# Storing 116-row output tiles as 112 + 4 rows in a one-core streaming encoder step

## The reference, cut to what matters

```python
h = x + jnp.concatenate([attn_out, lru_out], axis=-1) @ w_out
hn = rmsnorm(h, norm_ffn_g)
y = h + jnp.square(jax.nn.relu(hn @ w_up)) @ w_down
...
y_prompt = rmsnorm(yp, final_norm_g)   # (1, 2048, 1024) float32
y_sample = rmsnorm(ys, final_norm_g)   # (1, 32, 1024) float32
```

## Time and profile before

| what | value |
|---|---|
| time of the runs, median of 3 | 2148.1 us (2146.77 to 2150.18) |
| the profiled execution's own time | 2146.69 us |
| its span in the profile | 2144.9 us |
| PE busy / PEld busy | 1983.0 us (92%) / 1878.0 us (88%) |
| DVE busy | 1527.9 us (71%) |
| ACT busy | 1011.2 us (47%) |
| POOL busy | 430.8 us (20%) |
| mean granted clock of TensorE | 0.967 of full speed |
| hardware queue, share of 16 engines | 74.3%, 493.38 MB |
| software queue (POOL's transfers) | 0.8%, 5.67 MB |

### The profile page before, as it was taken

The page is one execution under the profiler, slowest core; times in us unless marked ns, Lnnn a source line. Parts: engine busy times, 40 slices in busy tenths (PEclk is TensorE's granted clock), DMA queues, the critical chain, the costliest instruction groups (busy, mean ns, idle before and its releaser), DMA issues.

```text
span 2144.9 us, 34224 instructions
## 1 busy us (share of the span) xinstructions
PE 1983.0 (92%) x11669; PEld 1878.0 (88%) x11669; DVE 1527.9 (71%) x2183; ACT 1011.2 (47%) x1967; POOL 430.8 (20%) x393
## 2 busy tenths in 40 slices
PE   6789889988987989999999989999999899999994
PEld 6778778777776779999999889999999799999994
DVE  7767867777678788878887966667767766666663
ACT  5555454544544555555555534433335533333331
POOL 3536656555567100100000001000000000000000
PEclk9889999999999999999999999999999999999997
DMA  6767676776755599989999887768878777777761
GB/s 178 226 174 225 176 238 197 209 234 192 214 188 161 167 300 316 317 287 298 345 326 299 290 270 243 230 205 267 272 220 269 239 213 217 216 217 216 216 211 63
DMA packets 396538, 500.91 MB, mean 234 GB/s; under 512 B 27498, under 2 KB 301450, under 8 KB 396394
## 3 DMA queue, kind: packets, MB, share of 16 engines
q1 hardware_dynamic: 394698, 493.38, 74.3%
q0 software_dynamic: 1696, 5.67, 0.8%
HBM read 375.36 MB, written 123.68 MB: 233 GB/s over the span
## 4 chain that ended last, share of the span: by engine, by line
PE 67%; DVE 10%; issue 8%; POOL 7%; DMA 3%; ACT 3%; SPq 1%; POOLq 0%; DVEq 0%; ACTq 0%
PE results L2056 19%; PE tail L2056 14%; PE scores_a L2056 14%; PE results L1840 10%; PE aux L2056 8%; DVE w_lo L1356 2%; PE aux L1960 1%; DVE hn_lo L1497 1%; POOL prob L929 1%; POOL xrow L898 1%; DMA out<-yout 1%; POOL xrow L902 1%; POOL xrow L900 1%; POOL third L900 1%; POOL sumsq L867 1%
## 5 line engine op out<-in xcount | busy, mean ns | idle before, releaser
L1035 ACT ACTIVATE w_hi<-w_raw 128x512 fp32r<-128x512 f32 (+1 forms) x360 | 240.8, 690 | 380.8 <-PE results L2056 160.5
L1507 DVE TENSOR_TENSOR w_lo<-w_raw,w_hi 128x512 fp32r<-128x512 f32 (+1 forms) x360 | 275.7, 779 | 49.0 <-ACT w_hi L1035 48.8
L1840 PE MATMUL results<-xg_hi,w_hi 128*128 128x448 f32 (+1 forms) x560 | 216.1, 386 | 27.6 <-DVE w_lo L1356 21.6
L1840 PE MATMUL results<-xg_lo,w_hi 128*128 128x448 f32 (+1 forms) x560 | 203.5, 363 | 0.0
L1840 PE MATMUL results<-xg_hi,w_lo 128*128 128x448 f32 (+1 forms) x560 | 203.0, 363 | 0.0
L2056 PE MATMUL results<-hn_hi,w_hi 128*128 128x348 f32 x576 | 187.4, 325 | 10.9 <-DVE x L1753 5.0
L971 ACT ACTIVATE w_hi<-raw 128x1024 fp32r<-128x1024 f32 x110 | 116.4, 1058 | 160.3 <-PE results L1840 156.8
L1356 DVE TENSOR_TENSOR w_lo<-raw,w_hi 128x1024 fp32r<-128x1024 f32 x110 | 155.4, 1413 | 49.5 <-ACT w_hi L971 49.5
L2056 PE MATMUL results<-hn_hi,w_lo 128*128 128x348 f32 x576 | 185.8, 323 | 0.0
L2056 PE MATMUL results<-hn_lo,w_hi 128*128 128x348 f32 x576 | 185.6, 322 | 0.0
L2056 PE MATMUL scores_a<-hn_hi,w_hi 128*128 128x348 f32 x480 | 155.8, 325 | 2.2 <-DVE x L1753 1.8
(11 more groups left out here) (274 smaller groups left out, 5665.7 us busy)
## 6 DMA issues: line engine op xcount, KB each, us to landing
w_lo<-s_scratch SPq DMA_DIRECT2D x128, 512.0 KB, 4.5
w_hi<-s_scratch SPq DMA_DIRECT2D x256, 256.0 KB, 3.5
w_raw<-in_w_up SPq DMA_DIRECT2D x144, 256.0 KB, 4.5
w_raw<-in_w_down SPq DMA_DIRECT2D x144, 256.0 KB, 4.3
raw<-in_w_in SPq DMA_DIRECT2D x70, 512.0 KB, 5.1
w_raw<-s_raw SPq DMA_DIRECT2D x64, 512.0 KB, 5.5
s_scratch<-w_lo SPq DMA_DIRECT2D x64, 512.0 KB, 5.9
s_scratch<-w_hi SPq DMA_DIRECT2D x128, 256.0 KB, 6.0
```

The lines of the kernel that those rows point to most:

```text
L1035: nc.scalar.activation(ring(w2_hi, u, ks[0], len(ks)), raw_slots(u, ks[0], len(ks)), ACT.Copy)\
L1507: nc.vector.tensor_tensor(w2_lo[u.s][:, PHYS[ks[0]]:PHYS[ks[0]] + len(ks), :], raw_slots(u, ks[0], len(ks)), ring(w2_hi.bitcast(F32), u, k ...
L1840: last = nc.tensor.matmul(out, wt, x(kx), start=(start and i == 0 and part == 0), stop=(stop and i == len(ks) - 1 and part == 2))
```

## The change

The twelve stores of blocks 0 and 1 are issued in two parts each: 112 and 4 rows for the 116-row tiles, 64 and 48 rows for the 112-row tile. Each part adds 16 to the semaphore, so every count that waits on `y_stored` doubles. In the last block a store is cut at the largest multiple of 16 rows: 112 and 4 rows, and for tile 5 80 and 4 rows, beside the 32 sample rows, which stay one transfer. So POOL issues 24 stores instead of 12, and SP issues 13 instead of 7.

```diff
+YS = 112
...
                 sp.wait_ge(yout_done, 1 + YT * b + YLAST.index(r) + 1)
-                if r < YT - 1:
-                    sp.dma_start(y_prompt[0, at:at + YR, :], out).then_inc(y_last, 16)
-                else:
-                    rest = YR - SAMPLE
-                    sp.dma_start(y_prompt[0, at:SEQ, :], out[0:rest, :]).then_inc(y_last, 16)
-                    sp.dma_start(y_sample[0], out[rest:YR, :]).then_inc(y_last, 16)
+                end = YR if r < YT - 1 else YR - SAMPLE
+                full = end // 16 * 16
+                for rs in (slice(0, full), slice(full, end)):
+                    sp.dma_start(y_prompt[0, at + rs.start:at + rs.stop, :], out[rs, :]).then_inc(y_last, 16)
+                if r == YT - 1:
+                    sp.dma_start(y_sample[0], out[end:YR, :]).then_inc(y_last, 16)
...
-                sp.wait_ge(y_stored[j], 16 * YT // 2 * (NB2 - 1))
-            sp.wait_ge(y_last, 16 * (YT + 1))
+                sp.wait_ge(y_stored[j], 32 * YT // 2 * (NB2 - 1))
+            sp.wait_ge(y_last, 16 * (2 * YT + 1))
...
                 pool.wait_ge(yout_done, 1 + YT * b + r + 1)
-                nc.gpsimd.dma_start(y_prompt[0, at:at + rows, :], out[0:rows, :]).then_inc(y_stored[r % 2], 16)
+                full = YS if rows > YS else YS - 48
+                for rs in (slice(0, full), slice(full, rows)):
+                    nc.gpsimd.dma_start(y_prompt[0, at + rs.start:at + rs.stop, :], out[rs, :]).then_inc(y_stored[r % 2], 16)
...
-                    act.wait_ge(y_stored[r % 2], 16 * (YT // 2 * b + r // 2))
+                    act.wait_ge(y_stored[r % 2], 32 * (YT // 2 * b + r // 2))
...
-                        act.wait_ge(y_stored[1], 16 * YT // 2 * u.b)
+                        act.wait_ge(y_stored[1], 32 * YT // 2 * u.b)
...
-                        act.wait_ge(y_stored[0], 16 * YT // 2 * (b - 1))
+                        act.wait_ge(y_stored[0], 32 * YT // 2 * (b - 1))
```

## The result

The changed kernel takes 2128.67 us (median of 4 runs, 2127.55 to 2135.09) against 2149.14 us for the kernel before on the same chip.

The account below looks back on a forecast made before the run. PE, 92% busy, was taken to bound the whole span, with time to regain only where it stands still. 2146.69 - 17.7 (end) + 2.0 (block starts) = 2131.0, given as 2132 us for the median; range 2126 to 2140.

Parts of the forecast that it names:

- Confinement to four engines: Last block's stores: 116-row transfers use only four of 16 engines, about 100 GB/s; the change to 112 rows removes this.
- The 17.7 us at the end: End of the kernel, behind DVE's last tile: span ends at 2127.2 us, 17.7 us saved, bounds 16.0 to 20.0.
- Issuing on SP: Last block: six more issues at 0.32 to 0.34 us each, hidden under DVE except the last tile's; longer issues are backlog.
- The rival: Last block: SP's issuing becomes the bound at 1.12 us or more per issue, 10.4 us saved, 2140 us; chance 0.07.
- The block starts: ACT's five waits for POOL's stores: 2.0 us lost to the second parts, between -1.0 and 5.2.
- the price of 0.4 us per wait: Block starts: each of ACT's five waits grows 0.4 us from the second part's issue, bounds -0.2 and 1.04.
- the two that I named: Block starts: two POOL stores in the chain that ended last, 5.96 and 5.94 us from issue to landing.
- That POOL's stores are padded: Block starts: each 116-row store is padded to 16 engines of 8 rows, so it already uses nearly all engines.
- The drain did speed up: Answers a rival for the last block: the drain stays at 100 GB/s or four engines, 2150 us; chance 0.03.
- the fixed share of a landing: Block starts, rival: second part pays 2.95 us again at five waits, 14.7 us, giving 2145 us; chance 0.04.
- a whole one: Block starts, rival: second part lands a whole landing later, 5 x 5.9 = 29.5 us, giving 2160 us; chance 0.03.
- That the block starts gain too: Block starts, rival: stores land some 0.5 us earlier at five waits, 2.5 us gained, giving 2128 us; chance 0.05.

Follow-up runs that it names:

- POOL's half alone: Kernel before with only POOL's twelve stores split in two, last block as before: 2146.07 us against 2147.0, ratio 0.9988.
- the last block's half alone: Kernel before with only the last block's stores split as in the change, POOL's stores whole: 2127.36 us against 2147.0, ratio 0.9906.
- 58 + 58: Kernel before with each 116-row store of the last block in two 58-row parts, tile 5 and POOL as before: 2171.17 us in one run.
- the 128-row tiles: Kernel before with tiles of 128 rows stored whole, small tile last: 2126.95 us against 2149.18, ratio 0.9889; once more 2124.27 us, ratio 0.9879.
- 47 issues: Changed kernel with the last block's 112-row parts as seven 16-row parts, 80 rows as five: end 15.6 us behind DVE, whole time not given.
- 64 + 64: The 128-row tiles with each store of the last block cut into 64 and 64 rows: 2128.3 us in one run.

## Why the prediction was right

The time, 2128.67 us, lies in the range and 3 us below the forecast; by the ratio the gain is 18 us where 16 were forecast.

*Confinement to four engines* was the right reading of the share of 0.25, shown by POOL's half alone, the last block's half alone, and above all by 58 + 58.

*The 17.7 us at the end* came out as 17.6, partly by luck. I let the last tile's second issue begin 0.4 us behind DVE and land 4.1 us later. It began 0.55 us behind DVE and was landed 4.0 us later, but these were made up differently: the issue was held up for 1.92 us, to 2.5 us behind DVE, and SP waited 2.1 us more. What ended last was the drain of all 2.85 MB. It ran from 2116 us to nearly 2127, at some 290 GB/s while the engines were full. I had the drain only as a bound, at the 229 GB/s of the earlier trace rows, a window with a share of 0.78, some twelve engines; the rate with all of them is higher.

*Issuing on SP* costs 0.35 us at the median, and the long issues were backlog, as I read them: with the faster drain of the 128-row tiles all seven issues take 0.33 to 0.34 us. The rival needs 47 issues to come true.

*The block starts* are the term that was mis-sized: 2.0 us lost were forecast. The sum of the waits is 0.1 us longer by the means above, and POOL's half alone has a ratio of 0.9988 (0.9977 to 1.0). What failed is the price of 0.4 us per wait, near an issue of 0.52, and with it the reading that 112-row stores land no sooner. The DMA view of the changed kernel has the stores at the block starts with the median us from issue to landing:

```profile
out<-yout POOLq DMA_DIRECT2D x6, 448.0 KB, 5.0
...
out<-hid_y POOLq DMA_DIRECT2D x4, 448.0 KB, 4.1
...
out<-yout POOLq DMA_DIRECT2D x6, 16.0 KB, 5.9
```

Whole stores took 5.9 and 5.5 us, so the 112 rows land about 1 us sooner. The 4 rows, issued half a microsecond later, take as long as a whole store did and land last, in the twelve pairs 0.7 to 1.9 us behind the first part. A pair landed 5.9 us after its first issue in the mean; whole stores took 5.6 us before and 5.9 us in the kernel with 58 + 58. So the first part gives back about what the second one costs.

The chain of before holds all five stores behind ACT's waits, not only the two that I named (the others landed in 6.80, 4.64 and 4.09 us), so these waits do lie on the path that ended last, as I took them to.

That POOL's stores are padded, read from the packet count, holds: with the split the count should be 10 x (128 + 32) + 2 x (112 + 32) = 1888 if the 4 rows are padded to 16, and 1888 it is. On which engines they run no run shows directly; that their split brings nothing like the gain of the end fits nearly all of them.

*The rivals.* The drain did speed up. A second part's landing takes long, 5.9 us for 16 KB, but it ran beside the first one's and not behind it, so neither the fixed share of a landing nor a whole one was paid again. The Trainium skill's page "DMA: Bandwidth & Descriptors", section "Rules for kernel authors", advises against two transfers for disjoint partition halves, since both use the same 16 engines. Where 16 engines work anyway the runs agree: 64 + 64, run once, is 3.2 us slower at the end than 128 whole. Where the row count of the whole store left most engines idle, 112 + 4 saved 17.6 us. That the block starts gain too, 2.5 us by the rival, the waits do not show, and the 0 to 4.9 us of POOL's half leave it open.

## What to carry to other kernels

Look at the DMA share where only one kind of transfer runs: a steady 0.25 or 0.13 was a number of engines here, 4 or 2 of 16, and the row count of the transfer is the first thing to check. At the end of this kernel a tile whose rows fill the engines in one transfer was better than cutting off the odd rows, 3.0 us behind DVE against 5.4. A split that helps on one queue need not do anything on another: count the packets first to see how the transfers are laid out there.

## What the runs showed that was not expected

- Whole 128-row stores to HBM ran at 377 to 391 GB/s, 112-row stores and all cut ones at 256 to 330, with engines busy for 0.94 to 0.96 and 0.81 to 0.98 of the time. For the same 2.85 MB the engines were busy for 120 us in all with the 128-row tiles (72.6% of 10.3 us on 16 engines) and for 143 us with the change (69.2% of 12.9 us). The cause is open.
- Transfers of 16 rows kept the engines 0.74 to 0.77 busy while they moved only 132 to 153 GB/s: small transfers take engine time beyond their bytes.
- The waits before the hidden storage at the block starts are 5 to 7 us whether tile 5 goes as 448 KB in one, in two parts, or is only 208 KB. Nearly all of such a wait is the landing of that last store, 4.1 and 5.9 us for 448 KB before and 6.1 us in the median for 208 KB. Its size does not set it; what does was not tried.
